# The first dense layer in another order, a third set of expert pages, and router weights loaded in whole rows

## The reference, cut to what matters

```python
mod = cond @ w_ada[i] + b_ada[i]                       # 6 x 1024 columns
sh1, sc1, g1, sh2, sc2, g2 = split(mod, 6)
h = rmsnorm(x, g_norm1) * (1 + sc1) + sh1
# layer 0
ga, gb, q, k, v = split(h @ w_in_e, 5)                 # 512 columns each
u = dwconv(ga * sigmoid(gb), conv_a_w) + conv_a_b      # 31 taps
u = silu(layernorm(u, ln_a_g, ln_a_b))                 # mean and variance over 512 channels
q, k = axial_rope(q), axial_rope(k)                    # latent tokens alone
a = softmax(q1 @ k1.T / 8) - lam * softmax(q2 @ k2.T / 8)
o = rmsnorm(a @ v, subln_g) * (1 - lam_init)           # by head, 4 heads of 128
x = x + g1 * (concat([u, o]) @ w_out_e)
# both layers
h = rmsnorm(x, g_norm2) * (1 + sc2) + sh2
g = argmax(softmax(h @ w_rg + b_rg))                   # 1 of 4 groups
top2 of (h @ w_re[g] + b_re[g])                        # of 8 experts in it
y = sum(weight_e * (silu(h @ w_gate[e]) * (h @ w_up[e])) @ w_down[e])
x = x + g2 * y
```

## Time and profile before

| | before |
|---|---|
| median of 3 runs | 1968.13 us (1967.0 to 1976.59) |
| profiled execution: as a run, its span | 1974.81 us, 1972.8 us |
| granted clock of TensorE, mean | 0.913 |
| TensorE busy | 1565.3 us, 79% |
| VectorE busy | 603.5 us, 31% |
| ScalarE, Pool busy | 233.6 us (12%), 213.5 us (11%) |
| moved by DMA | 558.92 MB, mean 283 GB/s |

### The profile page before, as it was taken

The page is one execution under the profiler, slowest core; times in us unless marked ns, Lnnn a source line. Parts: engine busy times, 40 slices in busy tenths (PEclk is TensorE's granted clock), DMA queues, the critical chain, the costliest instruction groups (busy, mean ns, idle before and its releaser), DMA issues. The chain is left out here.

```text
span 1972.8 us, 18415 instructions
## 1 busy us (share of the span) xinstructions
PE 1565.3 (79%) x6508; PEld 714.8 (36%) x6508; DVE 603.5 (31%) x1147; ACT 233.6 (12%) x448; POOL 213.5 (11%) x337
## 2 busy tenths in 40 slices
PE   4899987769598877877778389999597888787872
PEld 1445534545443322322233144555442233232330
DVE  1469545543521111211111432023521112111114
ACT  2111133311100000000000121101100000000001
POOL 0022010000011111111111000000021111111110
PEclk9999997869689999999999799999689899998996
DMA  8744202410569999999999655320679999999994
GB/s 303 237 146 178 86 11 86 150 43 31 204 271 419 421 420 421 421 421 420 419 418 413 257 200 213 129 107 31 246 280 421 420 420 420 420 418 415 421 393 185
DMA packets 125785, 558.92 MB, mean 283 GB/s; under 512 B 22877, under 2 KB 23702, under 8 KB 72234
## 3 DMA queue, kind: packets, MB, share of 16 engines
q1 hardware_dynamic: 96176, 518.64, 65.3%
q10 hardware_dynamic: 18170, 18.58, 2.9%
q0 software_dynamic: 11392, 21.08, 2.9%
HBM read 546.63 MB, written 26.28 MB: 290 GB/s over the span
## 5 line engine op out<-in xcount | busy, mean ns | idle before, releaser
L1453 PE MATMUL psum_pair_B<-weight_ring,scratch 128*64 128x512 f32 x2176 | 537.6, 651 | 138.0 <-DMA weight_ring<-w_up 127.0
L1453 PEld LDWEIGHTS psum_pair_B<-weight_ring,scratch 128*64 128x64 f32 x2176 | 181.5, 149 | 489.4 <-issue 486.0
L1471 PE MATMUL psum_pair_C<-weight_ring,scratch 128*64 128x512 f32 x1088 | 248.4, 597 | 38.5 <-issue 36.1
L1116 DVE TENSOR_TENSOR scratch<-psum_pair_B,scratch 128x256 f32<-128x256 f32 x68 | 28.9, 424 | 652.9 <-ACT scratch L728 652.9
L570 POOL DMA_INDIRECT expert_rows<-scratch,scatter_rows x68 | 69.5, 1022 | 848.6 <-DVE scratch L1128 848.6
L1368 PE MATMUL psum_pair_A<-scratch,weight_ring 128*128 128x128 f32 (+1 forms) x512 | 141.7, 435 | 2.5 <-DVE scratch L952 2.5
L1368 PE MATMUL psum_pair_B<-scratch,weight_ring 128*128 128x128 f32 (+1 forms) x512 | 143.6, 439 | 0.0
L1471 PEld LDWEIGHTS psum_pair_C<-weight_ring,scratch 128*64 128x64 f32 x1088 | 85.8, 136 | 154.3 <-issue 154.3
L728 ACT ACTIVATE scratch<-psum_pair_B 128x256 f32<-128x256 f32 x68 | 26.0, 383 | 940.9 <-PE psum_pair_B L1453 940.9
L1179 DVE SCALAR_TENSOR_TENSOR weight_ring<-weight_ring,params 128x655 f32<-128x655 f32 x120 | 114.0, 950 | 5.0 <-DVE gates_by_token L921 0.9
L1368 PEld LDWEIGHTS psum_pair_B<-scratch,weight_ring 128*128 128x128 f32 x512 | 79.1, 192 | 70.7 <-issue 70.7
(11 more groups left out here) (273 smaller groups left out, 1284.2 us busy)
## 6 DMA issues: line engine op xcount, KB each, us to landing
weight_ring<-w_gate SPq DMA_DIRECT2D x68, 2048.0 KB, 18.2
weight_ring<-w_up SPq DMA_DIRECT2D x68, 2048.0 KB, 22.7
weight_ring<-w_down SPq DMA_DIRECT2D x68, 2048.0 KB, 22.8
weight_ring<-w_ada SPq DMA_DIRECT2D x24, 2048.0 KB, 8.9
weight_ring<-w_in_e SPq DMA_DIRECT2D x5, 2048.0 KB, 13.0
scratch<-expert_rows SPq DMA_DIRECT2D x10, 1024.0 KB, 9.1
weight_ring<-w_in_o SPq DMA_DIRECT2D x4, 2048.0 KB, 19.1
h_rows<-scratch ACTq DMA_DIRECT2D x10, 512.0 KB, 3.2
```

What stands on the lines that cost most here:

```text
L1453: ins = mm(PB[B_][CAP * q:CAP * (q + 1), 512 * par:512 * par + 512].rearrange("p (u n) -> p u n", u=2), XGT[par][:, at:at + CAP], w[:, :, ...
L1471: ins = mm(PB[C_][CAP * q:CAP * (q + 1), 512 * par:512 * par + 512], HIDT[par][:, at:at + CAP], wd[:, j, 512 * q:512 * (q + 1)], start=(j ...
```

## The change

1. **The start.** X is issued first, in five loads with a semaphore for each tile. Then come modulation pages 0, 2, 1, 3 with four bias buffers instead of two. TensorE turns `hT` chunks between the modulation products, and the scale is made in two halves, so that chunks 0 to 3 want only products 0 and 2.
2. **Router weights.** `tables_and_caches` loads the router weights as whole rows into scratch (`WRG`, `WRE`), and Pool copies them into their places in ten copies. The caches go ahead of them. The cosines and sines are no longer part of the first load of constants, and are loaded here (`angles_loaded`), so the list has 20 issues.
3. **k projections and conv.** The four modulation products of layer 1 move from attention between the projections of k. The cached keys are turned ahead of k. Pool adds the four channel groups of the conv, and later their squares, so mean and variance are two matmuls each. ScalarE takes the squares in four buffers. The SiLU of the conv moves ahead of the end of the values, behind the third.
4. **Attention.** ScalarE squares and sums each head behind its unit (`head_squares`), and the last multiplication is made head by head.
5. **Experts.** A third set of three slots lies in scratch (`THIRD`), expert e goes into set e mod 3 and waits for the block three before it (e - 2 in counted blocks). Expert 2's up and down pages are issued behind the logits and the storing of h2, its gate page behind the slot weights. The buffers of the blocks move to make room (`XG`, `XGT` into `GW`, temporaries of the routing to scratch 0). ScalarE waits for the slot weights ahead of the first block. Semaphores `y_back` and `x_loaded` become `tile_in`. In layer 1 the load of `pool_w` moves behind the first norm.

The diff, cut to its core:

```diff
-        BIAS = [GW[:, 3072 + 512 * i:3584 + 512 * i] for i in range(2)]
+        BIAS = [GW[:, at:at + 512] for at in (3072, 3584, 0, 512)]
...
+        XG = [GW[:, 512 * i:512 * i + 512] for i in range(2)]
+        XGT = [GW[:, 1024 + 512 * i:1536 + 512 * i] for i in range(2)]
...
+        THIRD = 2560
...
-        dense = [[(0, ada(0, 0)), (1, ada(0, 1)), (2, ada(0, 2)), (3, ada(0, 3)),
+        dense = [[(0, ada(0, 0)), (1, ada(0, 2)), (2, ada(0, 1)), (3, ada(0, 3)),
...
-                  (0, mix("in_e", 4)), (1, ada(1, 0)), (2, mix("out_e", 0)), (3, mix("out_e", 1)),
-                  (1, ada(1, 1)), (1, ada(1, 2)), (1, ada(1, 3))],
+                  (0, mix("in_e", 4)), (1, ada(1, 0)), (1, ada(1, 1)), (1, ada(1, 2)), (1, ada(1, 3)),
+                  (2, mix("out_e", 0)), (3, mix("out_e", 1))],
...
-                        elif kind != 1:
-                            sp.wait_ge(sig("gate_up_done" if kind == 0 else "down_done", l), e - 1)
...
-                expert(0, 0, True)
-                expert(1, 1, True)
-                with nc.Fori(1, NE // 2, engines=(SP,)) as it:
-                    for par in range(2):
-                        expert(2 * it + par, par, False)
+                def load(e, st, kind):
+                    s = 3 * st + kind
+                    src = down_page(e) if kind == 2 else gate_page((wg, wu)[kind], e)
+                    sp.dma_start(gate_slot(s), src).then_inc(slot_full[s], 16)
+                def expert(e, st):
+                    sp.wait_ge(sig("gate_up_done", l), e - 2)
+                    load(e, st, 0)
+                    load(e, st, 1)
+                    sp.wait_ge(sig("down_done", l), e - 2)
+                    load(e, st, 2)
+                for s in range(4):
+                    page_free(sp, moe_base[l][1][s])
+                    load(s // 3, s // 3, s % 3)
+                page_free(sp, (("out_e", "out_o")[l], 1))
+                load(1, 1, 1)
+                load(1, 1, 2)
+                page_free(sp, ("logit", l))
+                sp.wait_ge(sig("h2_stored"), 16 * NT * (l + 1))
+                load(2, 2, 1)
+                load(2, 2, 2)
+                page_free(sp, ("weights", l))
+                load(2, 2, 0)
+                with nc.Fori(1, NE // 3, engines=(SP,)) as it:
+                    for st in range(3):
+                        expert(3 * it + st, st)
+                for e in range(NE - NE % 3, NE):
+                    expert(e, e % 3)
...
+            pool.wait_ge(sig("router_loaded"), 16 * 10)
+            for l in range(2):
+                pool.tensor_copy(WR[:, l, :, 0:NG], WRG[:, l])
+                for g in range(NG):
+                    ins = pool.tensor_copy(WR[:, l, :, NG + g * EPG:NG + (g + 1) * EPG], WRE[:, l, g])
+            link(ins)
...
+            for j in range(1, HC):
+                pool.wait_ge(sig("conv_step", j - 1), TAPS)
+                pool.wait_ge(sig("conv_step", j), TAPS)
+                link(pool.tensor_tensor(RS, UO[:, j], RS if j > 1 else UO[:, 0], ALU.add))
+            pool.sem_inc(sig("conv_summed"), 1)
+            for j in range(1, HC):
+                pool.wait_ge(sig("conv_squares"), j + 1)
+                link(pool.tensor_tensor(SQB[0], SQB[0], SQB[j], ALU.add))
+            pool.sem_inc(sig("squares_summed"), 1)
...
+                act.dma_start(SQ[:, 516:], a["const_square"][:, 516:]).then_inc(sig("angles_loaded"), 16)
...
-                    act.dma_start(WR[:, l, :, 0:NG], a["w_router_g"][l].rearrange("(p k) g -> p k g", k=DC)).then_inc(sig("tables_loaded"), 16)
+                    act.dma_start(WRG[:, l], a["w_router_g"][l].rearrange("(p k) g -> p k g", k=DC)).then_inc(sig("router_loaded"), 16)
                     for g in range(NG):
-                        act.dma_start(WR[:, l, :, NG + g * EPG:NG + (g + 1) * EPG],
-                                      a["w_router_e"][l, g].rearrange("(p k) e -> p k e", k=DC)).then_inc(sig("tables_loaded"), 16)
+                        act.dma_start(WRE[:, l, g], a["w_router_e"][l, g].rearrange("(p k) e -> p k e", k=DC)).then_inc(sig("router_loaded"), 16)
...
+                act.wait_ge(sig("row_weights"), l + 1)
...
+                    if (name, j) == ("k", 3):
+                        for i in range(HC):
+                            act.wait_ge(sig("centred"), i + 1)
+                            act.activation(SQB[i], UO[:, i, :], ACT.Square).then_inc(sig("conv_squares"), 1)
...
+            def head_squares(u):
+                t, h = UNITS[u]
+                after(act, "av", u)
+                act.activation(UP.rearrange("p j w -> p (j w)")[:, 128 * u:128 * (u + 1)], OR[:, t, h * 128:(h + 1) * 128], ACT.Square, accum_out=oss[:, 4 * t + h:4 * t + h + 1]).then_inc(sig("head_squares"), 1)
...
+            for j in range(HC):
+                dve.wait_ge(sig("conv_summed"), 1)
+                tt(UO[:, j, 0:NS], UO[:, j, 0:NS], MU[:, 0:NS], ALU.subtract)
+                tt(UO[:, j, 15 + NS:], UO[:, j, 15 + NS:], MU[:, NS:TOK], ALU.subtract).then_inc(sig("centred"), 1)
...
-            sq = PR.rearrange("p u c t -> p (u c t)")
-            flat = OR.rearrange("p t n -> p (t n)")
-            link(tt(sq, flat, flat, ALU.mult))
-            link(dve.tensor_reduce(oss, sq.rearrange("p (u e) -> p u e", e=128), AX_X, ALU.add))
+            dve.wait_ge(sig("head_squares"), NU)
...
-            tt(o3, o3, orstd.unsqueeze(2).broadcast_to([128, 20, 128]), ALU.mult).then_inc(sig("o_normed"), 1)
+            scale4 = orstd.rearrange("p (t h) -> p t h", h=HEADS)
+            for h in range(HEADS):
+                o3 = OR[:, :, h * 128:(h + 1) * 128]
+                tt(o3, o3, scale4[:, :, h:h + 1].broadcast_to([128, NT, 128]), ALU.mult).then_inc(sig("o_normed"), 1)
...
+            w = page(pe, ("in_e", 3))
+            for j in range(HC):
+                project(w, j, "k", j)
+                ada_products(1, j)
+                if j == 1:
+                    pe.wait_ge(sig("conv_summed"), 1)
+                    sum_of_channels("mean", RS)
+                if j:
+                    turned_sums(1, j - 1)
```

405 lines of the change are left out of this document (200 added, 205 removed).

## The result

| | before | after |
|---|---|---|
| median | 1972.24 us (4 runs, 1967.0 to 1976.59) | 1907.48 us (4 runs, 1905.92 to 1910.03) |
| profiled execution: as a run, its span | 1974.81 us, 1972.8 us | 1905.92 us, 1904.1 us |
| ratio of the times | | 0.9683, 95% interval 0.9657 to 0.9708 |

The change makes the kernel 3.2% faster, 65 us by the medians. The forecast was 1879 us in a range of 1863 to 1901, so the direction was right and the gain too large by 28.5 us. The kernel came out above the range.

The account below looks back on a forecast made before the run. Experts were taken as bound by transfers, the first dense part as a chain of small waits. Terms of -61.1 us there and -28.0 for the rings, together -89, took 1968.1 to 1879 us, range 1863 to 1901.

Parts of the forecast that it names:

- The start: Up to the first projection: it waits for both its pages and begins at 46 us instead of 58.5, -12.5 us.
- To attention: First projection to attention: less router-load waiting, variance and mean, more modulation products and turns, 2.3 us wait for Pool; -5.4 us.
- the router loads: First projection to attention: whole-row router loads free ScalarE, removing 10.5 us of waiting and 1.6 of slower projection, -12.1 us.
- Pool's share: Pool beside the conv: half a microsecond for each of twelve instructions, 6 us, as a bound outside the sum.
- Into attention: Values to first exponents: the exponents' table load no longer waits for the SiLU of the conv output, -5.8 us.
- attention: Units 1 to 16: modulation work leaves, units come 4.42 us apart, ScalarE's square of each head is hidden, -31.2 us.
- behind it: After attention: two VectorE passes go and the last is cut in four, less 1.6 us for square and table load, -6.2 us.
- rival 1: Attention stays at the lower clock, some 1.2 us more in 15 units: +18, 1897 us; chance 10%.
- The second dense part: Between the two layers' experts: the combine and second dense part keep their order, 0 us.
- The rings: Experts: a third page set loads expert 2 ahead of block 0, -15.8 us in layer 0, -12.2 in layer 1, together -28.0.
- the first gather: Layer 1: up and down pages run over the first gather, so block 0 starts 3.6 us later.
- Rival 3: Experts: the third expert brings nothing because block 0 or the last block comes later: +28, 1907 us; chance 8%.

Follow-up runs that it names:

- e3: Changed kernel with VectorE making the first norm ahead of the parameter copies: first projection at 50.06 us instead of 52.99, whole 1906.28 us.
- e8: Changed kernel with e3's norm order, first modulation product ahead of the first hT turns, first projection waiting for its own page alone: first projection at 49.08 us.
- e10: Changed kernel with e8's start, an own buffer for the third parameter turn, and products placed where their pages come: first projection at 44.43, whole 1903.6 us.
- e5: Kernel before with only the router weights loaded as whole rows and copied by Pool: 1956.6 us against 1968.29, ratio 0.9948.
- e2: Changed kernel with the mean behind the third k projection and two bias sums inside the conv's last group: 1898.02 us.
- e6: Changed kernel with Pool's first two cosine products moved from beside the conv to behind its sums: conv 127.05 us instead of 128.84, whole 1912.14 us.
- e1: Changed kernel with TensorE waiting for pool_w only ahead of its first use: second dense stretch 281.31 us instead of 285.3, whole only 2 us shorter.
- e11: Changed kernel with e10's start, e2's later mean and e1's later pool_w wait: 1884.76 us, ratio to before 0.9569.
- e4: Changed kernel with the waits of a ring of two, so the third expert set is undone alone: 1936.21 us, ratio to before 0.9842.
- e13: Kernel of e10 with 6 unread matmuls where TensorE stands for the conv: 1893.72 us, 75.00 us from conv's end to attention against 80.71.

## Why the prediction was wrong, step by step

The forecast lies 28.5 us under the median. 6.7 us are no step of the kernel: the sum was made against a profiled execution of 1974.81 us, and then taken from a median of 1968.13, which became 1972.24 with a fourth run. Another 1.6 us are the changed kernel's median above its profiled execution. The other 20.4 us are terms.

- **The start, -12.5 forecast, -5.5 measured.** The step that failed is "the first projection waits for both its pages ... hidden under the pages". I let TensorE make the fourth modulation product when its page was in, at 34. In the new order each product stands behind turns that wait for a norm, a scale or a copy, and the norm itself stood on VectorE behind parameter copies. e3, e8 and e10 take these away one after another, and only in e10 is a page waited for. The bytes were 2 us short as well: gb's page landed at 48.0, not 46. That e10 starts at 44.4, near the 46, is no confirmation of the term, since it does not wait for that page.
- **To attention, -5.4 forecast, +3.0 measured.** The parts on the router loads are confirmed (e5, -13.1 by itself). The step that failed is "the conv ... should end 148 us behind the first projection", which rested on the conv's own time and on u being there at the old distance. It ended at 154.2: 2.6 us since the first projection took 11.48 instead of 8.89, 3.0 for Pool's instructions beside it, and 0.7 of idle time left. Another 2.2 us came behind it, 1.7 of them the product at the lower clock. The wait of 1.25 us ahead of the variance, which I had counted as gone, stayed. And TensorE's wait, 5.48 us instead of 2.3, stood at another place than I had named: at a PSUM pair freed by a bias sum queued behind the conv. I had listed what is queued behind TensorE's wait, but not what the change queues behind the conv on VectorE. e2 moves both, the mean and the bias sums, and gives back 7.9 us; how much either gives alone was not tried.
- **Pool's share.** The sum had nothing for what Pool does to the conv, and the bound had half a microsecond for each of twelve instructions. Both were wrong in kind: a step that meets a two-input product or add of Pool costs VectorE 0.9 us (e6), three of these came with the change, and the ten copies cost next to nothing. Together they are 3.0 us. That my bound of 6 held them is luck, since most of it was for the copies.
- **Into attention (-5.8, -4.7), attention (-31.2, -31.6), behind it (-6.2, -6.9).** Right. The units lie 4.41 us apart from unit 2 on, which fits ScalarE's square of a head being hidden, as argued. The clock did not stay low (rival 1): only unit 1 was slow. All this is read from the timelines; none of it was undone alone.
- **The second dense part, 0 forecast, +5.8 measured.** The step that failed is "keep their order: 0". The diff showed the load of `pool_w` moved behind the first norm, and I did not ask who waits for it. e1 shows the wait, 3.4 us. The rest is the slow projection, which e11 did not have and e1 and e5 did.
- **The rings, -28.0 forecast.** Block 0 to expert rows became 14.0 and 17.3 us shorter, less 1.6 in front of layer 1's block 0: -29.7. Undoing the set alone (e4) costs 28.7 us by the medians. In layer 0 1.8 us are missing at the very end: the last block waits for the block before it and not for a page, and that one took 8.78 us for gate and up instead of 7.09, at a granted clock of 0.81. In e13 it took 7.09, and the stretch was 548.0 instead of 550.0. The 3.6 us for the first gather were 0.4. That three pages are "half of what the gap could hold" was a slip without effect: at 15.8 us per expert the 53 us hold over three experts.
- **The rivals.** None of the five came. Rival 3 names 1907 us, where the result lies, but that is chance: its mechanism, a third expert that brings nothing, is refuted by e4. What came was not among the rivals: two waits that the change itself made, and the clock behind one of them.

The range failed because it was built from errors in sizes. The misses were waits in places that I had given zero or a small value, all with the same sign.

## What to carry to other kernels

When a step is moved, follow every semaphore and every buffer that it frees or fills, on the engine where it now stands in line: two of the misses here were a bias sum behind a long run of VectorE and a small load whose waiter stood too early. A chain across four engines is not bound by the bytes until a page shows up as a releaser in it. And an engine that arrives earlier at a wait that stays gains nothing, and on TensorE it can lose: price such a wait at its length and, as a bound, once more for the clock behind it (here 1.7 us in most executions and 5.7 in the worst).

## What the runs showed of the hardware

- A wait of 5.6 us on TensorE made the 13.7 us of work behind it, up to the end of the next projection, 5.7 us longer at a granted clock of 0.72 and 0.67, and six matmuls that nobody reads, 5.3 us in its place, took that away (e10, e13). Behind waits of 5.48 us in the changed kernel it cost only 1.7 us (one product of 3.62 instead of 1.92), and in e6 a wait of 3.69 us was followed by the same slow rows as in e10, so how much is lost differs between executions and does not follow the length of the wait; what decides it stays open.
- The same start took from 52.99 to 57.38 us in six executions of the same code. In the longest (e1) three of the four modulation products took 3.5 to 3.6 us, and the four together 12.65 us instead of 9.06, so most of its 4.4 us are the clock. In e6 (55.27) they took 9.84, and 1.9 of its 2.3 us were there before the first turn, since the parameter rows landed later. That one order of the start would keep the clock up was not tried.
- Pool's instruction with two SBUF inputs, met by a VectorE step with two, doubled the step: 1.89 instead of 0.90 us. Beside Pool's ten copies the steps took 0.90 to 0.93 us.
- The eight loads of expert router weights held ScalarE for 11.1 us as pieces of 32 bytes and for 4.1 us, 0.5 each, as rows of 256 bytes; with the other issues, some of which shortened too, ScalarE was free after 9.3 us instead of 22.5 (before, e5).
